# The head of a hybrid encoder block: input tiles loaded first, two scale quarters summed by TensorE from raw blocks, and a new order of the first units

## The chip, the cores and the metric

The kernel runs on one core of a Trainium2 chip. The metric is the device time of one execution in microseconds (us), lower is better; the figures of a kernel are the median, the lowest and the highest of its runs. The profile is one more execution, taken by the hardware profiler.

## What is computed

One layer of an encoder on x with 512 tokens of 1024 features, all in float32. For this change only the beginning matters:

```python
c_act = jax.nn.silu(c)
mods = jnp.split(c_act @ w_ada[l] + b_ada[l], N_MOD, axis=-1)
sh1, sc1, g1, sh2, sc2, g2, sh3, sc3, g3 = mods
h = modulate(rmsnorm(x, norm_g[l, 0]), sh1, sc1)      # h * (1 + sc1) + sh1
x = x + 0.5 * g1[:, None, :] * swiglu(h, w_ffn1_in[l], w_ffn1_out[l])
```

c has 1024 entries, w_ada is 1024 x 9216 (nine vectors of 1024), w_ffn1_in is 1024 x 5632. After that follow the mixer (HGRN2 heads and windowed attention with a relative bias and a sink logit) and a second SwiGLU.

## The kernel before

The 1024 features are eight tiles (d or k, 0 to 7) of 128, features on partitions, tokens on the free axis. A product of float32 accuracy is made of three products of rounded parts: high weight x high activation (`hi_hi`), low weight x high (`lo_hi`), high weight x low (`hi_lo`). ScalarE rounds (`w_hi`, `h_hi`), VectorE subtracts (`w_lo`, `h_lo`). Each engine runs its own list in the order in which it is written out by hand, with waits on semaphores between engines; nothing is planned at run time. All loads named here go through SyncE's queue in program order, except `rows` (biases and gains) and small stores, which ScalarE issues.

**The head** (65 us with unit 2) works up to the first two units of FFN 1 (unit 0 is a gate tile pair, unit 1 the matching up pair):

- `x_nat` (two halves of 1 MB) is turned by TensorE into `xT` (`turn_x`); its root mean square per token goes into `rms0` (`square`, sqrt, reciprocal), `xn` = x / rms is turned as well (`turn_xn`) into banks.
- The factor `fac` of feature tile d is (1 + scale + bias) x gain, and the scale is a column of c_act @ w_ada. It is made in three pieces: tiles 0 and 1 (quarter 0), 2 and 3 (quarter 1), 4 to 7 (half 1). VectorE multiplies each of the eight k blocks by its entry of `cact` and adds them (`quarter_step`, `scale_step`, all in `first_step`), and TensorE sums the result over partitions with a column of ones (`column_sums`). The semaphore `s_mm` counts the pieces made, `s_step` VectorE's steps. `first_factor` then makes `fac`, `first_hi` and `first_lo` the two parts of h for a tile, `first_t` a float32 copy (`tmod`).
- `hi_hi(u, tiles)`, `lo_hi`, `hi_lo` are the products of unit u over these feature tiles, with the shift left out; the shift is made in the same way (`shift_step`) and added later.
- `w_first[0]` and `w_first[1]` hold the weights of units 0 and 1; unit 0's first half is split early (`first_split`), the rest counts in `whi_done` and `wlo_done`.
- The relative bias rows (`relb`, `table`, line 2143) and the sink broadcast (line 2144) are two float32 products that later stages need; ScalarE copies them out as `row8` and `sink_b`.

On TensorE the head stands in this order (lines 2129 to 2232): the turn of `rows`, column sums of quarter 0, turns of x tiles 0 and 1, bias and sink products, turns of xn tiles 0 to 2, unit 0 over tiles 0 and 1, column sums of quarter 1, turns, unit 0 over tiles 2 and 3, unit 1 over tiles 0 to 3, turns, column sums of half 1, and so on to the end of unit 1.

A float32 product of 128 weight columns stands in the trace as two instructions, each with its own weight load: the 2 products of `column_sums` for a quarter are 4 instructions there, the 4 for a half 8. A turn is one instruction per 128 x 128 block, a rounded product one per 128 x 512 block.

Of the kernel before, what the change touches and what calls it, by code (L numbers as in the profile page):

```python
# [108 lines left out]
def build(nc, x, c, w_ada, b_ada, norm_g, w_ffn1_in, w_ffn1_out, w_ffn2_in, w_ffn2_out,  # L109
# [163 lines left out]
    with ctx:  # L273
# [473 lines left out]
        def _(a):  # L747
# [76 lines left out]
            a.wait_ge(rowpad_done, 1)  # L824
            a.dma_start(bias_rows.rearrange("(h j) -> h j", h=QH), row8[:]).then_inc(bias_stored, 16)
            evac_x(2)
            first_t(2)
            first_t(3)
            evac_x(3)
            evac_x(4)  # L830
# [1843 lines left out]
```

## Time and profile before

| | |
|---|---|
| median of 3 runs | 1036.09 us (1035.14 to 1036.89) |
| the profiled execution | 1035.85 us |
| its span, first to last instruction | 1034.0 us |
| outside the span | 1.85 us |
| PE busy | 1013.7 us, 98% of the span |
| VectorE (DVE) busy | 804.1 us, 78% |
| ScalarE (ACT) busy | 507.9 us, 49% |
| the head with units 0 to 2 (line 2038 begins) | 65.4 us |

Busy shares are averages over a thousand microseconds; the change lies in the first 45. So the table says only that TensorE is nearly never idle over the whole kernel, and what the head is worth is to be read from its timeline and its chain.

### The profile page before, as it was taken

The numbers are of one execution on the slowest core, as the hardware profiler recorded it, in microseconds if no ns is written. First come the engines' busy times: TensorE is split into PE (matmuls) and PEld (weight loads), VectorE is DVE, ScalarE is ACT, GpSimd is POOL, SyncE is SP. The second block draws the span as 40 slices with busy tenths as digits, with TensorE's granted clock in tenths as the row PEclk, the third lists the DMA queues.
The fourth block names the chain that finished last, engine by engine and source line by source line (L and its number), as shares of the span: only waits on it lengthen the run. The fifth ranks groups of instructions, "written<-read, shape, count | busy, mean of one in ns | idle before, by whom it ended". The sixth has DMA issues, their size and how long they took to land.

```text
span 1034.0 us, 16712 instructions
## 1 busy us (share of the span) xinstructions
PE 1013.7 (98%) x6238; PEld 897.7 (87%) x6238; DVE 804.1 (78%) x1188; ACT 507.9 (49%) x782; POOL 48.8 (5%) x33
## 2 busy tenths in 40 slices
PE   5999999999999999999999999999999999999998
PEld 3788999999888888878878888887999999988887
DVE  6889989988987789888788649579888888746533
ACT  4646555555222354683535773554555555522231
POOL 0000000000000050020200000320000000000000
PEclk9999999999999999999999999999999999999999
DMA  9643434343877442823120031222232332363312
GB/s 345 233 163 122 133 114 139 105 159 127 294 275 244 163 163 84 273 72 102 41 72 31 2 83 41 82 82 82 83 121 93 110 115 88 123 245 124 119 41 82
DMA packets 93811, 133.59 MB, mean 129 GB/s; under 512 B 10786, under 2 KB 77214, under 8 KB 93639
## 3 DMA queue, kind: packets, MB, share of 16 engines
q1 hardware_dynamic: 93438, 130.83, 38.0%
q10 hardware_dynamic: 328, 2.17, 0.6%
q8 instruction: 28, 0.46, 0.2%
q14 instruction: 17, 0.13, 0.0%
HBM read 130.88 MB, written 4.21 MB: 131 GB/s over the span
## 4 chain that ended last, share of the span: by engine, by line
PE 85%; DVE 8%; ACT 2%; POOL 2%; DMA 2%; issue 1%; SPq 0%; POOLq 0%; DVEq 0%; ACTq 0%
PE bank L2038 13%; PE bank L2040 13%; PE bank L2039 13%; PE bank L2286 11%; PE bank L2285 11%; PE bank L2284 11%; PE bank L2388 2%; DVE w_lo L1254 2%; PE bank L2489 2%; PE bank L2582 1%; PE bank L2475 1%; ACT w_hi L757 1%; PE bank L2175 1%; DVE tmod L1338 1%; PE bank L2161 1%
## 5 line engine op out<-in xcount | busy, mean ns | idle before, releaser
L757 ACT ACTIVATE w_hi<-w_raw 128x2048 fp32r<-128x2048 f32 x47 | 90.0, 1914 | 201.9 <-PE bank L2040 190.9
L1254 DVE TENSOR_TENSOR w_lo<-w_raw,w_hi 128x2048 fp32r<-128x2048 f32 x47 | 109.5, 2330 | 94.6 <-ACT w_hi L757 94.5
L2284 PE MATMUL bank<-t_hi,left_hi 128*128 128x256 f32 x544 | 154.0, 283 | 0.0
L2285 PE MATMUL bank<-t_lo,left_hi 128*128 128x256 f32 x544 | 154.0, 283 | 0.0
L2286 PE MATMUL bank<-t_hi,left_lo 128*128 128x256 f32 x544 | 153.9, 283 | 0.0
L2038 PE MATMUL bank<-a_hi,w_hi 128*128 128x512 f32 x352 | 137.7, 391 | 0.3 <-DVE w_lo L1254 0.3
L2040 PE MATMUL bank<-a_hi,w_lo 128*128 128x512 f32 x352 | 137.0, 389 | 0.0
L2039 PE MATMUL bank<-a_lo,w_hi 128*128 128x512 f32 x352 | 137.0, 389 | 0.0
L2038 PE MATMUL bank<-h_hi,w_hi 128*128 128x512 f32 x336 | 133.3, 397 | 0.8 <-DVE w_lo L1254 0.8
L2040 PE MATMUL bank<-h_hi,w_lo 128*128 128x512 f32 x336 | 130.9, 390 | 0.0
L2039 PE MATMUL bank<-h_lo,w_hi 128*128 128x512 f32 x336 | 130.8, 389 | 0.0
L2286 PE MATMUL bank<-h_hi,left_lo 128*128 128x256 f32 x408 | 115.5, 283 | 0.0
L2285 PE MATMUL bank<-h_lo,left_hi 128*128 128x256 f32 x408 | 115.5, 283 | 0.0
L2284 PE MATMUL bank<-h_hi,left_hi 128*128 128x256 f32 x408 | 115.5, 283 | 0.0
L926 ACT ACTIVATE left_hi<-s_raw 128x512 fp32r<-128x512 f32 x136 | 85.6, 630 | 54.1 <-PE bank L2286 28.5
L2284 PEld LDWEIGHTS bank<-t_hi,left_hi 128*128 128x128 f32 x544 | 104.4, 192 | 0.0
L2285 PEld LDWEIGHTS bank<-t_lo,left_hi 128*128 128x128 f32 x544 | 104.4, 192 | 0.0
L2286 PEld LDWEIGHTS bank<-t_hi,left_lo 128*128 128x128 f32 x544 | 104.4, 192 | 0.0
L1544 DVE TENSOR_TENSOR left_lo<-s_raw,left_hi 128x512 fp32r<-128x512 f32 x136 | 92.9, 686 | 5.0 <-ACT left_hi L926 3.8
L1544 DVE TENSOR_TENSOR left_lo<-w_raw,left_hi 128x512 fp32r<-128x512 f32 x102 | 67.5, 688 | 20.2 <-ACT left_hi L926 18.9
L2284 PEld LDWEIGHTS bank<-h_hi,left_hi 128*128 128x128 f32 x408 | 78.3, 192 | 0.1
L2285 PEld LDWEIGHTS bank<-h_lo,left_hi 128*128 128x128 f32 x408 | 78.3, 192 | 0.1
(313 smaller groups left out, 1893.3 us busy)
## 6 DMA issues: line engine op xcount, KB each, us to landing
w_raw<-in_w_ffn_in SPq DMA_DIRECT2D x42, 1024.0 KB, 4.9
ada<-in_w_ada SPq DMA_DIRECT2D x24, 1024.0 KB, 5.0
w_raw<-in_w_ffn_out SPq DMA_DIRECT2D x22, 1024.0 KB, 4.8
w_raw<-in_w_mix_in SPq DMA_DIRECT2D x11, 1024.0 KB, 5.1
shift_in<-in_w_ada SPq DMA_DIRECT2D x4, 1024.0 KB, 8.3
ada_row<-in_w_ada SPq DMA_DIRECT2D x8, 512.0 KB, 4.2
scale_in<-in_w_ada SPq DMA_DIRECT2D x4, 512.0 KB, 6.9
x_nat<-in_x SPq DMA_DIRECT2D x2, 1024.0 KB, 9.0
```

The source lines that it names most:

```text
L757: sc.activation(w_hi[n % 2][:], src[:], ACT.Copy).then_inc(whi_done, 1)
L926: sc.activation(left_hi[p][:], left_source(f, u, p), ACT.Copy).then_inc(high_done, 1)
L1254: ve.tensor_tensor(w_lo[n % 2][:], src[:], as_f32(w_hi[n % 2][:]), ALU.subtract).then_inc(wlo_done, 1)
L1544: ve.tensor_tensor(left_lo[p][:], left_source(f, u, p), as_f32(left_hi[p][:]), ALU.subtract).then_inc(low_done, 1)
L2038: te.matmul(out_ap, wh, xh, start=first, stop=False)
L2039: te.matmul(out_ap, wh, xl, start=False, stop=False)
L2040: return te.matmul(out_ap, wl, xh, start=False, stop=last)
L2284: te.matmul(into, wh, xh[:, k, :], start=(opens and k == 0), stop=False, skip_group_check=True)
L2285: te.matmul(into, wh, xl[:, k, :], start=False, stop=False, skip_group_check=True)
L2286: ins = te.matmul(into, wl, xh[:, k, :], start=False, stop=(k == 3), skip_group_check=True)
L2388: ins = te.matmul(bank[4 + h][:, cols].rearrange("p (m two j) -> p m two j", two=2, j=b), kc(lev, h // GH)[:, h % GH, cols], alternate(q_b ...
L2489: ins = te.matmul(bank[4 + 2 * (n % 2) + g][:, j * (DH + 1):(j + 1) * (DH + 1)], pT[u % 4][:, i, :], av[:, key_first(n) + i, g, :], start= ...
```

## The change

The loads take a new order: both halves of x before the scale blocks, the first half of unit 0's weights after the first scale quarter, the second half of them last, behind the scale half. The two scale quarters are no longer multiplied and added by VectorE: TensorE multiplies each raw 128 x 128 block (as weights) by a column of `cact` (`direct_sums`), eight blocks for each of four feature tiles, accumulating in PSUM. The bias and sink products move from before the turns of xn to behind the first block of unit 0. Unit 1 over tiles 0 and 1 comes before unit 0 over tiles 2 and 3; `lo_hi(1, ...)` becomes one run before the column sums of the half instead of standing around them. ScalarE's and VectorE's lists follow.

```diff
+        SINK_SUM = bank[7][:, 32:32 + QH]
+        SCALE_SUMS = (bank[7][:, 0:1], bank[0][:, 0:1], bank[7][:, 2:3], bank[7][:, 3:4])
...
-            load_scale(0, 0)
-            load_scale(0, 1)
             for half in range(2):
                 sp.dma_start(x_nat[:, 2 * half:2 * half + 2, :],
...
+            load_scale(0, 0)
+            load_scale(0, 1)
+            load_w(0, slice(0, 4), first_ready[6])
             sp.dma_start(sink_r[:], attn_sink).then_inc(bias_consts, 16)
...
-            load_w(0, slice(0, 4), first_ready[6])
-            load_w(0, slice(4, DT), raw_ready[0])
             load_scale(1, 0)
             load_scale(1, 1)
             load_w(1, everything, raw_ready[1])
             load_scale_half(0)
             load_scale_half(1)
+            load_w(0, slice(4, DT), raw_ready[0])
...
+            square(0)
             a.wait_ge(vec_step, 1)
             sc.activation(vec[:], bank[0][:, 0:P], ACT.Copy).then_inc(vec_step, 1)
-            square(0)
...
-            a.wait_ge(sink_step, 1)
-            sc.activation(sink_b[:], bank[0][:, 0:QH], ACT.Copy).then_inc(sink_step, 1)
             evac_x(0)
+            evac_x(1)
             a.wait_ge(first_ready[6], 16)
...
+            a.wait_ge(sink_step, 1)
+            sc.activation(sink_b[:], SINK_SUM, ACT.Copy).then_inc(sink_step, 1)
             a.wait_ge(bias_mm, 1)
             sc.activation(row8[:], bank[3][0:QH, :], ACT.Copy).then_inc(rowpad_done, 1)
-            evac_x(1)
+            evac_x(2)
+            whi(1)
             first_hi(2)
             first_hi(3)
-            whi(1)
...
-            v.wait_ge(c_step, 2)
-            for k in range(DT):
-                quarter_step(0, k)
+            v.sem_inc(s_step, 16)
             square(1)
             v.wait_ge(vec_step, 2)
             ve.tensor_scalar(modv[:, DT:2 * DT], vec[:, DT:2 * DT], 1.0, None, ALU.add).then_inc(lb_dve, 1)
-            v.wait_ge(lb_dve, 1)
-            v.wait_ge(s_mm, 1)
-            first_factor((0, 1), (bank[7][:, 0:1], bank[7][:, 1:2]))
             square(3)
...
+            v.wait_ge(lb_dve, 1)
+            v.wait_ge(s_mm, 1)
+            first_factor((0, 1), SCALE_SUMS[0:2])
             v.wait_ge(first_split, 1)
             split_first(slice(0, 4 * 2 * P))
             first_lo(0)
             first_lo(1)
-            for k in range(DT):
-                quarter_step(1, k)
-            scale_step(0)
+            v.wait_ge(c_step, 2)
+            v.wait_ge(whi_done, 1)
+            ve.tensor_tensor(w_lo[1][:], w_first[1][:], as_f32(w_hi[1][:]), ALU.subtract).then_inc(wlo_done, 1)
             v.wait_ge(s_mm, 2)
...
+            def direct_sums(q, order):
+
+                for k, i in order:
+                    if i == order[0][1] and k % 4 == 0:
+                        pe.wait_ge(first_ready[2 * q + k // 4], 16)
+                    ins = te.matmul(SCALE_SUMS[2 * q + i], scale_in[q][:, k, i * P:(i + 1) * P], cact[:, k:k + 1],
+                                    start=(k == 0), stop=(k == DT - 1))
+                ins.then_inc(s_mm, 1)
...
+            direct_sums(0, [(k, i) for k in range(DT) for i in range(2)])
             pe.wait_ge(norms[0].rt, 2)
...
+            te.matmul(SINK_SUM, ones[0:1, :], sink_r[:], start=True, stop=True).then_inc(sink_step, 1)
+            te.matmul(bank[3][0:QH, :], relb[:], table[:], start=True, stop=True).then_inc(bias_mm, 1)
+            pe.wait_ge(sink_step, 2)
+            direct_sums(1, [(k, i) for i in range(2) for k in range(DT)])
+            pe.wait_ge(xT_act, 2)
+            pe.wait_ge(rowpad_done, 1)
+            pe.wait_ge(whi_done, 1)
+            hi_hi(1, (0, 1))
+            hi_lo(1, (0, 1))
```

The first place is TensorE's list from the turn of `rows` to the end of unit 0's first block. The numbers behind `quarter_acc` and `scale_in` are the quarters (98 and 89 quarter 0, 99 and 90 quarter 1), `w_hi_77` and `w_lo_79` are unit 0's weights. Before:

```order
L2130 MATMUL bank<-ident,rows 128x128
L2125 MATMUL bank<-ones,quarter_acc_98 128x1 x2
L2112 MATMUL bank<-ident,x_nat 128x128 x8
L2143 MATMUL bank<-table,relb 8x512
L2144 MATMUL bank<-sink_r,ones 128x8
L2112 MATMUL bank<-ident,xn 128x128 x12
L2161 MATMUL bank<-h_hi,w_hi_77 128x512 x4
L2167 MATMUL bank<-h_hi,w_lo_79 128x512 x4
L2175 MATMUL bank<-h_lo,w_hi_77 128x512 x4
L2125 MATMUL bank<-ones,quarter_acc_99 128x1 x2
```

The same stretch of TensorE's list in the change:

```order
L2110 MATMUL bank<-ident,x_nat 128x128 x4
L2141 MATMUL bank<-ident,rows 128x128
L2110 MATMUL bank<-ident,x_nat 128x128 x4
L2132 MATMUL bank<-cact,scale_in_89 128x1 x16
L2110 MATMUL bank<-ident,xn 128x128 x12
L2163 MATMUL bank<-h_hi,w_hi_77 128x512 x4
L2169 MATMUL bank<-h_hi,w_lo_79 128x512 x4
L2177 MATMUL bank<-h_lo,w_hi_77 128x512 x4
```

Two products ahead of the turns of xn have become sixteen, and the bias and sink products are gone from there.

The second place is TensorE's list behind that block, up to the column sums of the scale half (`w_hi_78`, `w_lo_80` are unit 1's weights). Before:

```order
L2112 MATMUL bank<-ident,xn 128x128 x4
L2112 MATMUL bank<-ident,x_nat 128x128 x4
L2161 MATMUL bank<-h_hi,w_hi_77 128x512 x4
L2167 MATMUL bank<-h_hi,w_lo_79 128x512 x4
L2175 MATMUL bank<-h_lo,w_hi_77 128x512 x4
L2161 MATMUL bank<-h_hi,w_hi_78 128x512 x8
L2175 MATMUL bank<-h_lo,w_hi_78 128x512 x8
L2112 MATMUL bank<-ident,xn 128x128 x4
L2112 MATMUL bank<-ident,x_nat 128x128 x8
L2167 MATMUL bank<-h_hi,w_lo_80 128x512 x4
L2125 MATMUL bank<-ones,scale_acc 128x1 x4
L2167 MATMUL bank<-h_hi,w_lo_80 128x512 x4
```

In the change the stretch begins so:

```order
L2110 MATMUL bank<-ident,xn 128x128 x4
L2110 MATMUL bank<-ident,x_nat 128x128 x4
L2193 MATMUL bank<-sink_r,ones 128x8
L2194 MATMUL bank<-table,relb 8x512
L2132 MATMUL bank<-cact,scale_in_90 128x1 x16
L2163 MATMUL bank<-h_hi,w_hi_78 128x512 x4
L2177 MATMUL bank<-h_lo,w_hi_78 128x512 x4
L2163 MATMUL bank<-h_hi,w_hi_77 128x512 x4
```

and ends so:

```order
L2163 MATMUL bank<-h_hi,w_hi_78 128x512 x4
L2177 MATMUL bank<-h_lo,w_hi_78 128x512 x4
L2110 MATMUL bank<-ident,x_nat 128x128 x8
L2169 MATMUL bank<-h_hi,w_lo_80 128x512 x8
L2123 MATMUL bank<-ones,scale_acc 128x1 x4
L2110 MATMUL bank<-ident,xn 128x128 x8
```

Eighteen small products stand ahead of unit 1's first four, and between the scale half's sums and the next unit-0 product only eight turns are left.

The third place is VectorE's list behind `first_lo` of tiles 0 and 1 (`TENSOR_TENSOR w_lo_80` is the low part of unit 1's weights). Before, with the semaphores that each row waits for:

```order
L1372 TENSOR_SCALAR quarter_acc_99<-scale_in_90,cact 128x256 [waits ada_first_ready2]
L1375 SCALAR_TENSOR_TENSOR quarter_acc_99<-scale_in_90,cact,quarter_acc_99 128x256 [waits s_step] x3
L1375 SCALAR_TENSOR_TENSOR quarter_acc_99<-scale_in_90,cact,quarter_acc_99 128x256 [waits s_step,ada_first_ready3]
L1375 SCALAR_TENSOR_TENSOR quarter_acc_99<-scale_in_90,cact,quarter_acc_99 128x256 [waits s_step] x3
L1372 TENSOR_SCALAR scale_acc<-scale_half_91,cact 128x512 [waits ada_first_ready4]
L1396 SCALAR_TENSOR_TENSOR fac<-bank,modv,vec 128x1 [waits s_mm]
L1396 SCALAR_TENSOR_TENSOR fac<-bank,modv,vec 128x1
L1414 SCALAR_TENSOR_TENSOR h_lo<-bank,fac,h_hi 128x512 [waits n0_hi] x2
L1375 SCALAR_TENSOR_TENSOR scale_acc<-scale_half_91,cact,scale_acc 128x512 [waits s_step] x2
L1455 TENSOR_TENSOR w_lo_80<-w_first_102,w_hi_78 128x2048 [waits whi_done]
```

In the change:

```order
L1447 TENSOR_TENSOR w_lo_80<-w_first_102,w_hi_78 128x2048 [waits whi_done,c_step]
L1398 SCALAR_TENSOR_TENSOR fac<-bank,modv,vec 128x1 [waits s_mm]
L1398 SCALAR_TENSOR_TENSOR fac<-bank,modv,vec 128x1
L1416 SCALAR_TENSOR_TENSOR h_lo<-bank,fac,h_hi 128x512 [waits n0_hi] x2
L1374 TENSOR_SCALAR scale_acc<-scale_half_91,cact 128x512 [waits ada_first_ready4]
L1377 SCALAR_TENSOR_TENSOR scale_acc<-scale_half_91,cact,scale_acc 128x512 [waits s_step] x3
```

Eight steps are gone, and the subtraction for unit 1's weights now stands ahead of the second `fac`.

## Rows read from the trace of the kernel before

**Rows 1.** The page, parts 1 and 2: busy time, granted TensorE clock.

```profile
PE 1013.7 (98%) x6238; PEld 897.7 (87%) x6238; DVE 804.1 (78%) x1188; ACT 507.9 (49%) x782; POOL 48.8 (5%) x33
...
PEclk9999999999999999999999999999999999999999
```

**Rows 2.** Stretches of the head: length, busy time per engine, PEclk, DMA share, GB/s.

```profile
13.30:19.90 6.60, 6.16 (x21) 3.73 (x21) 4.77 (x8) 4.99 (x9) 0.00 (x0) 1.00 1.09 387
19.90:27.00 7.10, 5.61 (x24) 4.26 (x24) 5.68 (x13) 3.42 (x7) 0.00 (x0) 1.00 1.05 409
27.00:43.00 16.00, 15.74 (x82) 12.46 (x82) 14.21 (x21) 9.92 (x15) 0.00 (x0) 1.00 0.63 215
```

**Rows 3.** Timeline of PE, 9 to 27 us: start, length of the group, instructions.

```profile
9.76 0.98 PE L2125 MATMUL bank<-ones,quarter_acc 128*128 128x1 f32 x4
...
13.26 1.12 PE L2112 MATMUL bank<-ident,x_nat 128*128 128x128 f32 x4 [1.46 <-DMA x_nat<-in_x]
14.30 1.87 PE L2143 MATMUL bank<-table,relb 33*8 33x512 f32 x2
...
16.63 2.82 PE L2112 MATMUL bank<-ident,xn 128*128 128x128 f32 x12
19.89 2.04 PE L2161 MATMUL bank<-h_hi,w_hi 128*128 128x512 f32 x4 [0.44 <-ACT h_hi L787]
21.73 1.33 PE L2167 MATMUL bank<-h_hi,w_lo 128*128 128x512 f32 x4
22.91 1.07 PE L2175 MATMUL bank<-h_lo,w_hi 128*128 128x512 f32 x4
25.21 0.61 PE L2125 MATMUL bank<-ones,quarter_acc 128*128 128x1 f32 x4 [1.24 <-DVE quarter_acc L1375]
...
27.04 1.30 PE L2161 MATMUL bank<-h_hi,w_hi 128*128 128x512 f32 x4 [0.28 <-ACT h_hi L787]
```

**Rows 4.** Timeline of PE, 31 to 39 us.

```profile
31.84 1.98 PE L2175 MATMUL bank<-h_lo,w_hi 128*128 128x512 f32 x8
...
36.02 1.05 PE L2125 MATMUL bank<-ones,scale_acc 128*128 128x1 f32 x8
...
37.94 1.03 PE L2112 MATMUL bank<-ident,xn 128*128 128x128 f32 x8
38.73 1.32 PE L2161 MATMUL bank<-h_hi,w_hi 128*128 128x512 f32 x4
```

**Rows 5.** Timeline of DVE, 10 to 36 us.

```profile
10.66 1.23 DVE L1408 CUSTOM_DVE_ANT_0 xn<-x_nat 128x1024 f32<-128x1024 f32 x1 [1.05 <-DMA x_nat<-in_x]
...
13.24 1.23 DVE L1408 CUSTOM_DVE_ANT_0 xn<-x_nat 128x1024 f32<-128x1024 f32 x1 [0.88 <-DMA x_nat<-in_x]
...
15.05 2.08 DVE L1440 TENSOR_SCALAR xn<-x_nat,rms 128x1024 f32<-128x1024 f32 x3
...
21.49 3.67 DVE L1375 SCALAR_TENSOR_TENSOR quarter_acc<-scale_in,cact,quarter_acc 128x256 f32<-128x256 f32 x7
...
25.86 0.34 DVE L1396 SCALAR_TENSOR_TENSOR fac<-bank,modv,vec 128x1 f32<-128x1 f32 x2 [0.30 <-PE bank L2125]
...
29.80 2.28 DVE L1455 TENSOR_TENSOR w_lo<-w_first,w_hi 128x2048 fp32r<-128x2048 f32 x1
32.00 3.96 DVE L1375 SCALAR_TENSOR_TENSOR scale_acc<-scale_half,cact,scale_acc 128x512 f32<-128x512 f32 x5
```

**Rows 6.** Timeline of ACT, 19 to 29 us.

```profile
19.06 1.27 ACT L787 ACTIVATE h_hi<-bank,fac 128x512 fp32r<-128x512 f32 x2 [0.72 <-PE bank L2112]
...
21.81 0.57 ACT L817 ACTIVATE row<-bank 8x512 f32<-8x512 f32 x1
...
26.30 0.69 ACT L787 ACTIVATE h_hi<-bank,fac 128x512 fp32r<-128x512 f32 x1 [3.44 <-DVE fac L1396]
...
27.45 1.91 ACT L757 ACTIVATE w_hi<-w_first 128x2048 fp32r<-128x2048 f32 x1
```

**Rows 7.** The last stretch of the span, columns as in group 2.

```profile
1032.00:1034.00 2.00, 0.00 (x0) 0.00 (x0) 0.00 (x0) 0.00 (x0) 0.00 (x0) 0.65 0.52 155
```

More of the change, by code:

```diff
@@ L815, in _ @@
             first_t(1)
+            a.wait_ge(sink_step, 1)
+            sc.activation(sink_b[:], SINK_SUM, ACT.Copy).then_inc(sink_step, 1)
             a.wait_ge(bias_mm, 1)
             sc.activation(row8[:], bank[3][0:QH, :], ACT.Copy).then_inc(rowpad_done, 1)
-            evac_x(1)
+            evac_x(2)
+            whi(1)
             first_hi(2)
             first_hi(3)
-            whi(1)
+            first_t(2)
+            first_t(3)
+            a.wait_ge(rowpad_done, 1)
+            a.dma_start(bias_rows.rearrange("(h j) -> h j", h=QH), row8[:]).then_inc(bias_stored, 16)
+            evac_x(3)
+            evac_x(4)
             a.wait_ge(raw_ready[0], 16)
             sc.activation(w_hi[0][:, 4 * 2 * P:], w_first[0][:, 4 * 2 * P:], ACT.Copy).then_inc(whi_done, 1)
[L824 to L830, printed above, removed]
             first_hi(4)
@@ L1444, in _ @@
             first_lo(1)
-            for k in range(DT):
-                quarter_step(1, k)
-            scale_step(0)
+            v.wait_ge(c_step, 2)
+            v.wait_ge(whi_done, 1)
+            ve.tensor_tensor(w_lo[1][:], w_first[1][:], as_f32(w_hi[1][:]), ALU.subtract).then_inc(wlo_done, 1)
             v.wait_ge(s_mm, 2)
-            first_factor((2, 3), (bank[7][:, 2:3], bank[7][:, 3:4]))
+            first_factor((2, 3), SCALE_SUMS[2:4])
             first_lo(2)
             first_lo(3)
-            scale_step(1)
-            scale_step(2)
-            v.wait_ge(whi_done, 1)
-            ve.tensor_tensor(w_lo[1][:], w_first[1][:], as_f32(w_hi[1][:]), ALU.subtract).then_inc(wlo_done, 1)
+            for k in range(3):
+                scale_step(k)
             for k in range(3, DT):
@@ L2127, in column_sums @@
                 ins.then_inc(s_mm, 1)
-            pe.wait_ge(rows_loaded, 16 * 6)
-            te.transpose(bank[0][:, 0:P], rows[:], ident[:]).then_inc(vec_step, 1)
-            pe.wait_ge(pool_set, 7)
-            column_sums(8, quarter_acc[0], 0, 2)
+            def direct_sums(q, order):
[5 more added lines that the diff above has]
+                ins.then_inc(s_mm, 1)
             pe.wait_ge(x_loaded[0], 16)
@@ L2136, in _ @@
             turn(bank[2], x_nat, 1, (0, 1))
+            pe.wait_ge(rows_loaded, 16 * 6)
+            te.transpose(bank[0][:, 0:P], rows[:], ident[:]).then_inc(vec_step, 1)
             pe.wait_ge(x_loaded[1], 16)
@@ L2139, in _ @@
             turn(bank[2], x_nat, 1, (2, 3)).then_inc(x_tr, 1)
-            pe.wait_ge(bias_consts, 48)
             pe.wait_ge(vec_step, 2)
-            te.matmul(bank[3][0:QH, :], relb[:], table[:], start=True, stop=True).then_inc(bias_mm, 1)
-            te.matmul(bank[0][:, 0:QH], ones[0:1, :], sink_r[:], start=True, stop=True).then_inc(sink_step, 1)
+            direct_sums(0, [(k, i) for k in range(DT) for i in range(2)])
             pe.wait_ge(norms[0].rt, 2)
@@ L2177, in hi_lo @@
                 return ins
-            pe.wait_ge(sink_step, 2)
             pe.wait_ge(xT_act, 1)
@@ L2185, in _ @@
             hi_lo(0, (0, 1))
-            column_sums(16, quarter_acc[1], 2, 2)
             pe.wait_ge(norms[0].t, 1)
@@ L2190, in _ @@
             turn_x(2)
+            pe.wait_ge(pool_set, 7)
+            pe.wait_ge(bias_consts, 48)
+            te.matmul(SINK_SUM, ones[0:1, :], sink_r[:], start=True, stop=True).then_inc(sink_step, 1)
[7 more added lines that the diff above has]
+            hi_lo(1, (0, 1))
             hi_hi(0, (2, 3))
@@ L2193, in _ @@
             hi_lo(0, (2, 3))
-            pe.wait_ge(xT_act, 2)
-            pe.wait_ge(rowpad_done, 1)
-            pe.wait_ge(whi_done, 1)
-            hi_hi(1, range(4))
-            hi_lo(1, range(4))
             pe.wait_ge(xT_act, 3)
             turn_xn(4)
+            hi_hi(1, (2, 3))
+            hi_lo(1, (2, 3))
             pe.wait_ge(norms[0].t, 4)
@@ L2204, in _ @@
             pe.wait_ge(wlo_done, 1)
-            lo_hi(1, (0, 1))
+            lo_hi(1, range(4)).then_inc(first_used, 1)
             column_sums(24, scale_acc, 4)
-            lo_hi(1, (2, 3)).then_inc(first_used, 1)
             pe.wait_ge(xT_act, 5)
```

## The prediction, made before the changed kernel ran

> **What bounds the kernel now.** The page says that TensorE (PE) is busy for 98% of the span [rows 1], so over the whole kernel a delay of PE is a delay of the end. In the head this holds only from some point on, and the stretches show from where: PE is busy for 5.61 of 7.10 us from 19.9 to 27 us, and for 15.74 of 16.00 us from 27 to 43 us [rows 2]. So from 27 us PE sets the pace, and what counts is when it gets there and with how much work left. The timeline of PE shows what it waits for before: the second half of x (13.26 us), ScalarE's first `h_hi` (19.89 us), VectorE's second scale quarter (25.21 us, after 1.24 us idle), and `h_hi` of tile 2 (27.04 us) [rows 3]. Nothing behind 27 us has a stall that takes up a delay, so a shift there is taken as passed on in full.
>
> One more thing is to be seen in group 3: PE is slow at first. The granted clock is listed as full, 1.00, in every stretch of the head [rows 2], but the rows disagree with it: from the start of four 128x512 products to the next row it takes 1.84 us at 19.89 us, of which a part is a wait; the later ones cost (1.98 - 1.07) / 4 = 0.23 us each [rows 3, 4]. The small float32 column products say it more cleanly: four take 0.98 us at 9.76 us and 0.61 us at 25.21 us, eight take 1.05 us at 36.02 us [rows 3, 4]. That is (1.05 - 0.61) / 4 = 0.11 us each at full rate, with a tail of 0.28 us, and (0.98 - 0.3) / 3, about 0.22 us, at half rate; I use 0.213, half of the 0.427 us that a half-rate 128x512 product would take. The change to full rate falls into the second row of unit 0's block (21.73 us: 1.33 us for four, the next four 1.07 us) [rows 3]. Before it PE had been busy without a break from 13.26 to 19.4 us, with turns, the 33-row bias product and the sink, and this did not raise the rate; it rose a little over 2 us into the 128x512 products.
>
> **The change, part by part.** I follow PE, which runs its list in order, and call E the moment at which unit 0's first block (twelve 128x512 instructions) is out: before, 22.91 + 4 x 0.227 = 23.8 us [rows 3].
>
> Loads. The halves of x landed at 10.66 and 13.24 us, 2.58 us for 1 MB, with the DMA engines full at 387 GB/s [rows 2, 5]. With x ahead of the 1 MB of scale quarter 0, x is there at about 8.1 and 10.7 us, and the quarter's two halves at about 11.95 and 13.24 us. xn was finished 17.13 - 13.24 = 3.9 us after the second half of x [rows 5], so now at 14.6 us. Nothing later in the queue is short: unit 1's weights come 2.5 MB later, at about 20 us, and the postponed second half of unit 0's weights at about 26.5 us, needed after 37 us.
>
> First sum on PE. Sixteen products are 32 instructions. They start with the first half quarter at 11.95 us and run without a gap, since the second half lands before the first sixteen are through: 32 x 0.213 = 6.8 us, to 18.8 us. I take PE to stay at half rate through it, as it did through the thin products and turns before. The turns of xn stand behind them in the list and start at 19.0 us instead of 16.63 us [rows 3]: xn waits 4.4 us for PE. The bias and sink products, 2.33 us there before (14.30 to 16.63 us), are gone, and this is in the 19.0. So the early x buys nothing: **+2.4 us**. From there to E all is as before: ten turns, `h_hi` at +2.43 us [rows 3, 6], the block. E becomes 26.2 us.
>
> From E on. Before, the products of unit 0 over tiles 2 and 3 started at 27.04 us, E + 3.2 [rows 3]. Now ahead of them stand: eight turns 0.87 us (eight took 0.79 at 37.94 us [rows 4]); the sink and bias products, half of 2.33 us at full rate, 1.15; 32 instructions of the second sum at 0.11, 3.5; and eight products of unit 1 pulled forward, 8 x 0.227 = 1.81 [rows 4]. That is E + 7.3. But `h_hi` of tile 2 comes later still, by a chain across the engines: the bias product ends at E + 2.2, ScalarE copies `row8` and evacuates x tile 2 (0.5 us each, as the 0.57 us row), then rounds unit 1's weights (1.91 us [rows 6]), to E + 5.1; VectorE's list has the subtraction for these weights (2.28 us, 2.2 to the next [rows 5]) ahead of the second `fac`, so that `fac` starts at E + 7.4 although the sum is there at E + 5.5; from `fac` to PE it takes 27.04 - 25.86 = 1.18 us [rows 3, 5]. So PE starts at **E + 8.55** and idles 1.2 us. Of these 8.55 us 1.81 are work done in advance. Net: 8.55 - 3.2 - 1.8 = **+3.5 us**. A cheaper second sum would not help, since it is not on this chain; a half-rate one would.
>
> The scale half. Before, from the start of its column sums (36.02 us) to the next unit-0 product (38.73 us) were 2.71 us, filled by the sums 0.9, four `lo_hi` 0.9 and eight turns 0.8 [rows 4]. The four `lo_hi` now stand ahead. The path (sums, four `fac`, `h_hi`) stays 2.71 us, the cover shrinks by 0.9: **+0.9 us** of idle. The eight steps of VectorE before it start at E + 9.9, cost about 0.78 us each (3.96 us for five [rows 5]), and end at E + 15.7; PE comes to the sums at E + 16.5, so they are just not late. If they were, each microsecond would count in full.
>
> VectorE. Sixteen steps of 0.5 us (seven in 3.67 us [rows 5]) are gone. Of the first eight none was on the path; the other eight were the 1.24 us wait of PE, which is in the E + 3.2. The rest of the relief lands in waits for `s_mm` and for the weights' rounding, so it counts nothing more. ScalarE's `square(0)` ahead of `vec` costs nothing: `vec` is needed at 11.95 us by the first sum, and both are through by 10.3 us. The later shift loads wait for `s_mm` and `xn_tr` and move with PE, and their users move too.
>
> Sum: 2.4 + 3.5 + 0.9 = **+6.8 us** on the profiled 1035.85 us (span 1034.0 and 1.85 around it), 1042.7 us; the median of the runs, 1036.09, stands 0.24 higher, which I leave within the rounding.
>
> What a thin product costs the rows show: 0.11 and 0.21 us for exactly this form, each instruction with its own 128-column weight load [rows 3, 4]. The Trainium skill (TensorE: Matmul & The Clock Gate, Back-to-back issue gap) gives about 25 ns as the floor of a product with few columns. By it the first sum would be 32 x 0.025 = 0.8 us and the turns would start when xn is ready, at 14.6 us, 2 us earlier than before: -2.0 + 3.5 + 0.9 = +2.4 us, an estimate from that page. The trace does not agree with so low a price.
>
> **The rivals.**
> - The rate rises during the first sum. For it: 6.8 us of instructions back to back, each with a full weight load. Against it: the same kind of continuous row between 13.26 and 19.4 us did not do it. If it rises in mid-sum, around 17 us, the sum ends at 18.0, the turns and the block run at full rate (1.3 and 2.7 us), and E is about 23.1 us: -0.7 + 4.4 = +3.7 us, 1039.6 us (1038.7 to 1040.4 by the moment).
> - The rate falls again behind the first block. From E to E + 5.5 there are only turns, thin products and the second sum. Before, 3.2 us of that kind passed without harm [rows 3]; but at the end of the kernel, when only turns were left, the granted clock fell, 0.65 on average over the last 2 us [rows 7]. Then a rest of the second sum, the eight pulled products and a part of the next block run at half rate: about 1 + 0.4 + 1.3 us more, +9.5 us, 1045.4 us. The Trainium skill (same page, HAM oscillation) warns of this, gaps between bursts of products that put the clock back; no row before shows it in the head.
> - PE at full rate nearly from the start: the first sum ends at 15.0 us, the block at 20.2 us, -3.6 + 4.4 = +0.8 us, 1036.7 us: no change. The rows at 9.76 and 19.89 us speak against it.
> - Faster: the head's end is set by VectorE and not by PE. Then x 2.6 us earlier and eight steps less (4.1 us) count, -6.7 us, the chain behind E gives back 3.5: -3.2 us, 1032.7 us. It decides if VectorE has less idle time than PE between 27 and 43 us; it was busy for 14.21 of 16 us against PE's 15.74 [rows 2], so I give it little.
>
> **How the numbers follow.** Half rate through the first sum, no fall: 0.45. Fall behind the block: 0.20. Rise in mid-sum: 0.17. No change: 0.11. Faster: 0.07. The likeliest gives 1042.7 us, by itself 1041.5 to 1044 (when in the block the rate rises, up to 1 us; 0 to 0.9 us for the scale half). For eight in ten the range takes in the mid-sum rise and the fall: 1037.9 to 1046.5 us. 0.2% is 2.07 us, about what a measurement of this kernel can tell from no change; the first three cases are slower by more, 0.82, with a little of the third kept back: slower 0.81, same 0.12, faster 0.07.
>
> **What would show it.** In the changed profile: 32 instructions of line 2132 at about 0.21 us from 12 to 19 us; the first turn of xn near 19.0 us; the first `h_hi` product near 22.3 us; the second sum at 0.11 us each; VectorE's second `fac` directly behind the subtraction of unit 1's weights, and PE idle for about 1.2 us before unit 0's tiles 2 and 3; about 0.9 us idle behind the scale half's sums; the first product of line 2036 near 72.2 us instead of 65.4. I am wrong if the rate is up before 17 us, if a 128x1 instruction on raw blocks costs less than 0.1 us, or if the delay of the head is not found again at the end.

## The result, and the profile after

The changed kernel takes **1042.08 us** (median of 4 runs, 1041.37 to 1042.87), the kernel before 1036.07 us in the same comparison. The ratio is 1.0059, with a 95% interval of 1.0047 to 1.0071: slower by 6.0 us. The profiled execution is one of 1041.37 us with a span of 1039.6 us, 5.6 us more than before.

Parts 1 and 2 of the page after, to be read beside [rows 1]:

```profile
PE 1023.4 (98%) x6294; PEld 908.7 (87%) x6294; DVE 803.2 (77%) x1172; ACT 507.8 (49%) x782; POOL 49.0 (5%) x33
...
PEclk9899999999999999999999999999999999999999
```

TensorE has 56 instructions and 9.7 us of busy time more, VectorE 16 instructions less. That is the exchange which the change makes: 64 thin instructions on PE in place of 8 and of sixteen steps of VectorE. And one digit of the granted clock is new: the second fortieth of the span, which ends at 52 us, has an 8 where before a 9 stood. Where in it the clock is low, the stretches show (length, busy time of PE, PEld, DVE, ACT, POOL, then PEclk, DMA share, GB/s):

```profile
11.90:20.00 8.10, 8.10 (x39) 8.10 (x40) 3.28 (x6) 2.79 (x4) 0.00 (x0) 1.00 1.08 391
20.00:27.00 7.00, 6.56 (x36) 4.44 (x34) 1.41 (x2) 3.66 (x7) 0.00 (x0) 1.00 1.06 404
27.00:36.00 9.00, 9.00 (x39) 8.08 (x39) 5.85 (x8) 4.61 (x6) 0.00 (x0) 0.62 0.38 142
36.00:46.00 10.00, 9.37 (x56) 7.85 (x55) 6.79 (x14) 3.42 (x6) 0.00 (x0) 1.00 0.23 76
71.00:1039.60 968.60, 961.66 (x5996) 857.37 (x5994) 759.72 (x1104) 471.12 (x727) 47.97 (x22) 1.00 0.36 120
```

Before, the clock stood at 1.00 in every stretch of the head [rows 2]. Now it averages 0.62 from 27 to 36 us, where PE is busy for 9.00 of 9.00 us: the busy time looks perfect, and for three quarters of it (27.7 to 34.5 us) PE runs at 1.2 GHz. The other stretches read 1.00. That can't be trusted before 20.88 us: a group of four turns takes 1.11 us there and 0.60 at 23.79 us, so PE is at half rate while the listing says 1.00, as in the kernel before.

The timeline of PE (start, length of the group, what it is, idle time before it), to be read beside [rows 3, 4]:

```profile
6.90 1.11 PE L2110 MATMUL bank<-ident,x_nat 128*128 128x128 f32 x4 [3.64 <-DMA x_nat<-in_x]
9.41 1.12 PE L2110 MATMUL bank<-ident,x_nat 128*128 128x128 f32 x4
10.82 6.96 PE L2132 MATMUL bank<-cact,scale_in 128*128 128x1 f32 x32 [0.29 <-DMA scale_in<-in_w_ada]
17.64 2.80 PE L2110 MATMUL bank<-ident,xn 128*128 128x128 f32 x12
20.88 1.22 PE L2163 MATMUL bank<-h_hi,w_hi 128*128 128x512 f32 x4 [0.44 <-ACT h_hi L789]
...
23.79 0.60 PE L2110 MATMUL bank<-ident,xn 128*128 128x128 f32 x4
...
25.07 1.02 PE L2194 MATMUL bank<-table,relb 33*8 33x512 f32 x2
26.02 5.50 PE L2132 MATMUL bank<-cact,scale_in 128*128 128x1 f32 x32
31.38 2.05 PE L2163 MATMUL bank<-h_hi,w_hi 128*128 128x512 f32 x4
33.23 1.68 PE L2177 MATMUL bank<-h_lo,w_hi 128*128 128x512 f32 x4
34.74 1.08 PE L2163 MATMUL bank<-h_hi,w_hi 128*128 128x512 f32 x4
...
44.99 1.22 PE L2163 MATMUL bank<-h_hi,w_hi 128*128 128x512 f32 x4 [0.63 <-ACT h_hi L789]
71.57 0.39 PE L2036 MATMUL bank<-h_hi,w_hi 128*128 128x512 f32 x1
```

The three landmarks of the prediction: E, the end of unit 0's first block, is at 23.79 us, where it was before (23.8). Unit 0's products over tiles 2 and 3 begin at 34.74 us instead of 27.04. The head ends at 71.57 us instead of 65.40, +6.17 us. The same 128x512 products cost 1.08 us a group of four from 34.74 us, 2.05 at 31.38 us: there the half rate is visible in the rows too.

VectorE and ScalarE, whose rows answer to [rows 5, 6]:

```profile
11.62 2.08 DVE L1437 TENSOR_SCALAR xn<-x_nat,rms 128x1024 f32<-128x1024 f32 x3
17.90 0.34 DVE L1398 SCALAR_TENSOR_TENSOR fac<-bank,modv,vec 128x1 f32<-128x1 f32 x2 [4.19 <-PE bank L2132]
29.09 2.29 DVE L1447 TENSOR_TENSOR w_lo<-w_first,w_hi 128x2048 fp32r<-128x2048 f32 x1 [6.91 <-ACT w_hi L759]
31.55 0.34 DVE L1398 SCALAR_TENSOR_TENSOR fac<-bank,modv,vec 128x1 f32<-128x1 f32 x2 [0.17 <-PE bank L2132]
```

```profile
20.05 1.27 ACT L789 ACTIVATE h_hi<-bank,fac 128x512 fp32r<-128x512 f32 x2 [5.36 <-PE bank L2110]
26.13 0.59 ACT L820 ACTIVATE row<-bank 8x512 f32<-8x512 f32 x1 [0.77 <-PE bank L2194]
27.10 1.89 ACT L759 ACTIVATE w_hi<-w_first 128x2048 fp32r<-128x2048 f32 x1
```

xn is ready at 13.7 us and waits until 17.64 us for PE. The relieved VectorE stands idle for 4.19 us in front of the first `fac` and 6.91 us in front of `w_lo`. So the time that it was spared shows as waiting.

### The profile page after: what moved, and what is told of

It reads as the page before. It is cut to its first block, busy times and chain, and to the rows that moved or that the text cites. A ratio compares the mean times of both kernels' runs of the same rounds, so it can differ in the third digit from the quotient of the medians.

```text
span 1039.6 us, 16807 instructions
## 1 busy us (share of the span) xinstructions
PE 1023.4 (98%) x6294; PEld 908.7 (87%) x6294; DVE 803.2 (77%) x1172; ACT 507.8 (49%) x782; POOL 49.0 (5%) x33
## 4 chain that ended last, share of the span: by engine, by line
PE 89%; DVE 7%; ACT 1%; issue 1%; DMA 1%; SPq 0%; DVEq 0%; ACTq 0%
PE bank L2036 14%; PE bank L2038 14%; PE bank L2037 14%; PE bank L2293 11%; PE bank L2292 11%; PE bank L2291 11%; PE bank L2395 2%; PE bank L2496 2%; PE bank L2589 1%; DVE w_lo L1256 1%; PE bank L2163 1%; PE bank L2132 1%; PE bank L2177 1%; PE bank L2482 1%; PE bank L2169 1%; DVE tmod L1340 1%
## 5 line engine op out<-in xcount | busy, mean ns | idle before, releaser
L2036 PEld LDWEIGHTS bank<-a_hi,w_hi 128*128 128x128 f32 x352 | 66.1, 188 | 14.2 <-DVE w_lo L1256 0.7
```

The source lines that it names most:

```text
L2036: te.matmul(out_ap, wh, xh, start=first, stop=False)
```

## The experiments

Each kernel was timed beside the kernel before, in 5 to 11 runs; the median of the kernel before was 1035.86 to 1035.95 us in these comparisons. The table orders them by what they start from. "Head" is the start of the first product of `stage_k8` in the profiled execution (65.40 us in the kernel before), E and "tiles 2/3" are the landmarks above.

| kernel | E | tiles 2/3 | head | median us | ratio (95%) |
|---|---|---|---|---|---|
| before | 23.8 | 27.04 | 65.40 | 1036.07 | |
| after | 23.79 | 34.74 | 71.57 | 1042.08 | 1.0059 (1.0047 to 1.0071) |
| e1_first_sum_cut | 19.98 | 30.43 | 67.77 | 1037.37 | 1.0016 (1.0007 to 1.0024) |
| e2_second_sum_cut | 24.01 | 33.02 | 70.45 | 1040.56 | 1.0048 (1.0035 to 1.0061) |
| e3_second_sum_dve | 24.12 | 33.12 | 71.07 | 1040.66 | 1.0045 (1.0032 to 1.0058) |
| e9_fill_wait | 24.66 | 32.01 | 68.91 | 1038.78 | 1.0031 (1.0019 to 1.0042) |
| e4_spin | 21.88 | 31.68 | 69.64 | 1040.50 | 1.0046 (1.0033 to 1.0059) |
| e5_old_tail | 25.33 | 29.38 | 69.19 | 1038.35 | 1.0022 (1.0013 to 1.0031) |
| e6_old_tail_spin | 22.25 | 26.30 | 66.17 | 1035.74 | 0.9999 (0.9990 to 1.0008) |
| e8_spin_fill | 25.59 | 29.89 | 69.44 | 1039.08 | 1.0020 (1.0011 to 1.0029) |
| e12_loads_only | 27.5 | 30.69 | 69.05 | 1039.40 | 1.0039 (1.0025 to 1.0052) |
| e10_bias_moved | 23.4 | 26.57 | 64.99 | 1035.60 | 0.9998 (0.9989 to 1.0007) |
| e11_bias_moved_spin | 21.6 | 25.95 | 65.41 | 1035.63 | 1.0000 (0.9991 to 1.0009) |
| e7_before_spin | 22.7 | 26.90 | 66.43 | 1035.45 | 0.9990 (0.9981 to 0.9999) |

Taken within one execution, the time of the profiled run less its head is 969.8 to 970.5 us for all fourteen kernels: a delay of the head is passed on to the end, within 0.8 us. A median can differ from the profiled execution by more (e5's was profiled in the slowest of its eleven runs, at 1039.05 us), so a difference is given by medians here, and by profiles where that is said.

**Which sum is on the path.** Two kernels keep the change and cut one of its two sums down to 4 of its 32 instructions, behind a wait for the same loads.

```diff
-            direct_sums(0, [(k, i) for k in range(DT) for i in range(2)])
+            pe.wait_ge(first_ready[1], 16)
+            direct_sums(0, [(0, i) for i in range(2)], 1)
```

> The changed kernel with the first direct sum cut from 32 instructions to 4 (only the first of the eight k blocks is multiplied, so the scale of tiles 0 and 1 is incomplete). Theory, the first sum lies whole on the path: xn is ready at 13.7 us and its turns start there and not at 17.6 us, and the kernel ends 3.0 to 4.0 us earlier than the changed one, at about 1038.5 us, still 2 to 3 us above the kernel before. Rival, the sum is covered by something else (weights, w_hi, the clock): the end moves by less than 1 us.

It measured 4.7 us less than after, a little above the 3.0 to 4.0 expected; by the two profiles it is 3.8. The turns of xn start at 13.32 us instead of 17.64:

```profile
12.48 0.99 PE L2132 MATMUL bank<-cact,scale_in 128*128 128x1 f32 x4 [1.69 <-DMA scale_in<-in_w_ada]
13.32 2.80 PE L2110 MATMUL bank<-ident,xn 128*128 128x128 f32 x12
```

The 28 missing instructions would have taken 28 x 0.213 = 6.0 us; 1.69 us of that is the wait for the second half of the quarter, now uncovered, and the 4.3 us that are left are found at the turns. The first sum stands wholly on the path.

The second kernel does the same to `direct_sums(1, ...)`, with a wait on `first_ready[3]`.

> The changed kernel with the second direct sum cut from 32 instructions to 4 (one of eight k blocks, so the scale of tiles 2 and 3 is incomplete). Theory, the chain bias product, row8, w_hi, w_lo, fac is next behind it: products of unit 0 over tiles 2 and 3 start 8.5 us after the first block's end and not 11 us, PE idles about 4 us in two places, and the kernel ends about 2.4 us earlier than the changed one, about 1039.7 us. Rival, only PE's time counts: 4.9 us of sum and 1.5 us of half-rate products go, 6.4 us, about 1035.7 us.

It measured 1.5 us less than after, so most of the second sum's 5.36 us was hidden, as the first theory has it. The size was 0.9 us off. PE's timeline shows the wait that takes its place:

```profile
26.24 0.61 PE L2132 MATMUL bank<-cact,scale_in 128*128 128x1 f32 x4
29.47 2.05 PE L2163 MATMUL bank<-h_hi,w_hi 128*128 128x512 f32 x4 [2.62 <-ACT w_hi L759]
31.31 1.91 PE L2177 MATMUL bank<-h_lo,w_hi 128*128 128x512 f32 x4
33.02 1.65 PE L2163 MATMUL bank<-h_hi,w_hi 128*128 128x512 f32 x4
```

The pulled-forward products of unit 1 wait 2.62 us for ScalarE's rounding of its weights. VectorE's second `fac` starts at 31.52 us, E + 7.5, directly behind `w_lo`. And the products of unit 1 run at half rate (2.05 and 1.91 us for four): the clock falls here without a second sum.

**The second sum back on VectorE, its `fac` ahead of `w_lo`.**

```diff
-            v.wait_ge(whi_done, 1)
-            ve.tensor_tensor(w_lo[1][:], w_first[1][:], as_f32(w_hi[1][:]), ALU.subtract).then_inc(wlo_done, 1)
+            for k in range(DT):
+                quarter_step(1, k)
             v.wait_ge(s_mm, 2)
             first_factor((2, 3), SCALE_SUMS[2:4])
+            v.wait_ge(whi_done, 1)
+            ve.tensor_tensor(w_lo[1][:], w_first[1][:], as_f32(w_hi[1][:]), ALU.subtract).then_inc(wlo_done, 1)
...
-            direct_sums(1, [(k, i) for i in range(2) for k in range(DT)])
+            column_sums(16, quarter_acc[1], 2, 2)
```

> The changed kernel with quarter 1 summed by VectorE again (eight steps of 0.5 us and two column sums), and the second fac ahead of the subtraction for unit 1's weights. Theory: the VectorE steps run while it would idle (7 us before its w_lo), fac waits no longer for w_lo, the clock has no long thin stretch in which to fall; ScalarE's rounding of unit 1's weights (to 5.1 us behind the block) is then what h_hi of tile 2 waits for, products over tiles 2 and 3 start some 6 us behind the block, and the end is about 5 us earlier than the changed kernel, 1037 us, within 0.2% of the kernel before. Rival, the second sum is not what costs: less than 2 us.

Only 1.4 us less than after, so this was a miss. `fac` comes at 26.99 us and is no longer in the way, but PE's own list is: unit 1's products stand ahead. PE waits 2.62 us for `w_hi`, then runs them at half rate, and tiles 2 and 3 start at E + 9.0 and not at about E + 6:

```profile
26.37 0.58 PE L2125 MATMUL bank<-ones,quarter_acc 128*128 128x1 f32 x4
29.57 2.05 PE L2165 MATMUL bank<-h_hi,w_hi 128*128 128x512 f32 x4 [2.62 <-ACT w_hi L759]
31.42 1.91 PE L2179 MATMUL bank<-h_lo,w_hi 128*128 128x512 f32 x4
33.12 1.91 PE L2165 MATMUL bank<-h_hi,w_hi 128*128 128x512 f32 x4
```

**Is it the clock?** e9 takes e3 and puts three products of a constant tile (each two instructions) into this wait.

```diff
             column_sums(16, quarter_acc[1], 2, 2)
+            pe.wait_ge(xT_act, 2)
+            for _ in range(3):
+                te.matmul(bank[2][:], ones[:], ones[:, 0:1].to_broadcast([P, TOK]), start=True, stop=True)
             pe.wait_ge(xT_act, 2)
```

> The kernel of e3_second_sum_dve with three extra 512-column products of ones (2.6 us at full rate) behind the column sums of quarter 1, where PE idled for 2.6 us until unit 1's weights were rounded. Theory, it is the thin and idle stretch behind the block, 5 us and more without 512-column products, in which the rate falls, and two stretches at half rate over real products cost 3.4 us: with the gap filled the rate stays up and the median falls from 1040.7 to about 1037.3 us. Rival, the fall has another cause or costs nothing: 1040.7 us or more.

It measured 1.9 us less than e3 with more work on PE. The stretch from 27 to 36 us, e3 first, then e9:

```profile
27.00:36.00 9.00, 6.43 (x16) 5.08 (x17) 6.78 (x10) 4.80 (x7) 0.00 (x0) 0.62 0.37 142
```

```profile
27.00:36.00 9.00, 9.00 (x38) 6.33 (x39) 6.34 (x9) 5.35 (x7) 0.00 (x0) 1.00 0.37 140
```

The granted clock is 0.62 in the one and 1.00 in the other. The timeline of PE in e9:

```profile
27.36 2.83 PE L2201 MATMUL bank<-ones 128*128 128x512 f32 x6
30.12 1.15 PE L2165 MATMUL bank<-h_hi,w_hi 128*128 128x512 f32 x4
31.11 1.07 PE L2179 MATMUL bank<-h_lo,w_hi 128*128 128x512 f32 x4
32.01 1.07 PE L2165 MATMUL bank<-h_hi,w_hi 128*128 128x512 f32 x4
```

The products of unit 1 start 0.55 us later than in e3 and are through 1.11 us sooner. So the fall is a cost of its own in this place. Two profiles alone would not show this, since in e9 the clock also rose later within the first block (E is 24.66 us, 24.12 in e3); but all seven runs of e9 (1037.88 to 1039.32 us) lie below all five of e3 (1039.96 to 1040.85).

**The fall without the new tail.** e5 keeps the new loads and the first sum, and puts everything behind the first block into the order of before, except that the bias and sink products stay behind the block.

```diff
-            direct_sums(1, [(k, i) for i in range(2) for k in range(DT)])
-            pe.wait_ge(xT_act, 2)
-            pe.wait_ge(rowpad_done, 1)
-            pe.wait_ge(whi_done, 1)
-            hi_hi(1, (0, 1))
-            hi_lo(1, (0, 1))
+            column_sums(16, quarter_acc[1], 2, 2)
             hi_hi(0, (2, 3))
             lo_hi(0, (2, 3))
             hi_lo(0, (2, 3))
```

> The changed kernel's loads and first sum on PE, and everything behind the first block of unit 0 as before (quarter 1 by VectorE, unit 0 over tiles 2 and 3 ahead of unit 1, ScalarE's rounding of unit 1's weights behind h_hi 2 and 3); bias and sink products stay behind the block. Theory, the tail order and its chain cost the changed kernel its 6 us and loads plus first sum cost nothing: products over tiles 2 and 3 start 4.0 us behind the block's end of 23.8 us, the rate does not fall since the thin stretch is 4 us and not 7.5, and the median is 1036 to 1037 us. If the rate falls all the same, it costs up to 3.4 us: 1039 to 1040 us. Rival, the first sum is the cost: 1040 us or more with no fall in the granted clock.

1038.35 us: with the loads, the first sum and the moved bias products alone the kernel is 2.4 us slower than before, and the new tail costs the other 3.6 of the 6.0. The start of tiles 2 and 3 came as expected, 4.05 us behind the block, but two parts missed: loads and first sum are not free, and the rate fell although the stretch without 128x512 products was 4 us long and not 7.6. In its timeline the full rate comes late, within the second row of the block (from 23.02 us), and tiles 2 and 3 start at E + 4.05:

```profile
21.17 2.04 PE L2166 MATMUL bank<-h_hi,w_hi 128*128 128x512 f32 x4 [0.44 <-ACT h_hi L789]
23.02 1.55 PE L2172 MATMUL bank<-h_hi,w_lo 128*128 128x512 f32 x4
...
29.38 1.31 PE L2166 MATMUL bank<-h_hi,w_hi 128*128 128x512 f32 x4 [1.22 <-ACT h_hi L789]
30.53 1.62 PE L2172 MATMUL bank<-h_hi,w_lo 128*128 128x512 f32 x4
31.95 1.91 PE L2180 MATMUL bank<-h_lo,w_hi 128*128 128x512 f32 x4
```

The clock falls within the row at 30.53 us, and the last row is at half rate: the granted clock is 0.81 from 27 to 36 us, low from 30.9 to 34.3 us. From the first of tiles 2 and 3 to the turns behind unit 1 (37.58 us) it takes 8.20 us, where before it took 6.62 [rows 3] (27.04 to 33.66 us), so the fall is 1.6 us of the 3.8 us by which this profile's head is longer. How much of the 2.4 us of the medians is the fall, no run separates.

Up to this block e5 and after have the same instructions on PE, and their turns of xn start within 0.3 us of each other; yet the block takes 4.16 us in the one and 2.91 in the other, and E differs by 1.5 us. When the rate rises varies that much between two executions.

**The loads alone.** e12 is the kernel before with only the order of loads changed.

```diff
-            load_scale(0, 0)
-            load_scale(0, 1)
             for half in range(2):
                 sp.dma_start(x_nat[:, 2 * half:2 * half + 2, :],
...
+            load_scale(0, 0)
+            load_scale(0, 1)
+            load_w(0, slice(0, 4), first_ready[6])
```

> The kernel before with the change's order of loads alone. Theory, without the sums on PE the early x is of no use: VectorE starts quarter 0's eight steps at 10.7 us instead of 5.5 us and squares and xn follow only then, PE waits with its column sums until 14.8 us, so h_hi comes about 2 us later, 1038 to 1039 us. Rival, the early x counts by itself: 1034 us.

+3.5 us, 0.4 more than the upper end expected. x first, and PE waits for VectorE instead, whose eight steps now stand behind the later quarter:

```profile
15.23 0.98 PE L2125 MATMUL bank<-ones,quarter_acc 128*128 128x1 f32 x4 [5.66 <-DVE quarter_acc L1375]
...
20.28 2.82 PE L2112 MATMUL bank<-ident,xn 128*128 128x128 f32 x12
```

The turns of xn start 3.65 us later than before, and tiles 2 and 3 also 3.65 us later. So the direct sum on PE makes the new load order bearable (e5, +2.4). Not run were the direct sum with the old loads, and the new loads with VectorE's squares ahead of its eight steps; what either costs is open.

**The bias products alone.** e10 is the kernel before with the bias and sink products behind the first block.

```diff
-            te.matmul(bank[3][0:QH, :], relb[:], table[:], start=True, stop=True).then_inc(bias_mm, 1)
-            te.matmul(bank[0][:, 0:QH], ones[0:1, :], sink_r[:], start=True, stop=True).then_inc(sink_step, 1)
...
             hi_lo(0, (0, 1))
+            te.matmul(SINK_SUM, ones[0:1, :], sink_r[:], start=True, stop=True).then_inc(sink_step, 1)
+            te.matmul(bank[3][0:QH, :], relb[:], table[:], start=True, stop=True).then_inc(bias_mm, 1)
```

> The kernel before with one part of the change alone: bias and sink products behind unit 0's first block (the sink sum in bank 7), their copies on ScalarE behind h_hi of tiles 3 and 2. They then fill the 1.2 us in which PE waits for quarter 1, and the turns of xn start at 15.8 us and not at 16.6 us. Theory: about 1 us earlier than before, 1035.0 us. Rival, the block starts in an earlier state of the clock or quarter 1's loads decide: no difference.

> The kernel of e10_bias_moved with the four extra products of ones at the start. Theory: the spin gave e7_before_spin 0.5 us, and here again about 0.5 us, 1034.5 us. Rival: more time without dense products, one more fall, 1036 us.

Head 0.4 us shorter in e10's profile, no difference in either time. The turns of xn start at 16.11 us, held up by ScalarE's part of xn and not by the products. So moved into PE's wait for VectorE they are free, and they were nearly free before. In e11 the block runs at full rate nearly from its start, but the clock falls again, from 25.6 to 29.0 us, over the products of tiles 2 and 3 (2.08 us for the first four, 1.30 in e10): the rival's fall is there, and the head ends where it did before.

**Full rate from the start.** Four kernels let PE run four products of a constant tile (`spin(1)`, and `spin(3)` behind the transposition of `c_row`) while it waits for the first loads: after, e5, before and e10 with this.

```diff
+            pe.wait_ge(pool_set, 2)
+            spin(1)
             pe.wait_ge(consts_loaded, 32)
             te.transpose(bank[2][:, 0:DT], c_row[:], ident[0:DT, 0:DT]).then_inc(c_step, 1)
+            spin(3)
```

> The changed kernel with four extra 512-column products of ones into an unused bank at the very start, while PE waits for the first loads. Theory, half rate is half the price of the first sum: if the rate is up when the sum starts at 10.8 us, its instructions cost 0.11 us and it ends 3.4 us earlier, and the kernel ends 2 to 4 us earlier, about 1039 us; if the rate falls within the sum, less. Rival, instructions on raw blocks are bound by their weight loads at any rate: the sum stays 6.8 us and the end does not move.

> The kernel of e5_old_tail with the four extra products of ones at the start. Theory, the half rate of the first sum and the first block is worth 3 us: if the rate is up at 10.6 us the sum ends at 14.6 us and the block 3 us earlier, 1033 to 1034 us; the rate can fall in the sum, and then half of that is lost, 1035 us. Rival, no gain against e5_old_tail.

> The kernel before with the same four extra products at the start and nothing else. Theory, only the stretch from 13.3 to 22.3 us gains from a full rate: turns, bias product and half of the first block, 1 to 3 us in all, but VectorE's second quarter follows its h_lo and so moves along: 1034 to 1035 us, and nothing if the rate has fallen again by 13 us, where PE waits for x. Rival, the weights and x decide and not the rate: no difference from before.

The gain is 1.6 us on after (its runs spread from 1038.14 to 1041.66), 2.6 on e5, 0.5 on before and none on e10. What limits it is seen in e6. PE's timeline, then its stretches:

```profile
10.92 4.13 PE L2143 MATMUL bank<-cact,scale_in 128*128 128x1 f32 x32 [0.76 <-DMA scale_in<-in_w_ada]
14.91 2.80 PE L2121 MATMUL bank<-ident,xn 128*128 128x128 f32 x12
18.16 2.04 PE L2174 MATMUL bank<-h_hi,w_hi 128*128 128x512 f32 x4 [0.44 <-ACT h_hi L789]
20.00 1.49 PE L2180 MATMUL bank<-h_hi,w_lo 128*128 128x512 f32 x4
```

```profile
14.90:20.00 5.10, 4.66 (x18) 3.90 (x18) 3.40 (x7) 2.44 (x4) 0.00 (x0) 0.50 1.08 395
27.00:31.00 4.00, 4.00 (x12) 3.20 (x12) 3.96 (x5) 4.00 (x5) 0.00 (x0) 0.59 0.91 325
```

The first sum takes 4.0 us instead of 6.8, because most of it runs at full rate. Then the clock falls at 14.0 us, so the turns and the first row of the block are as slow as in e5, and it falls once more behind the block, as in e5. The gain at the sum is kept and nothing is added to it: E, tiles 2 and 3 and the head are 3.1, 3.1 and 3.0 us earlier than in e5. On before it is otherwise. In e7 the block is through 1.1 us earlier, but tiles 2 and 3 still wait for VectorE and start at 26.90 us, and now the clock is low from 26.7 to 30.2 us, where before it was not: the four products there take 2.07 us instead of 1.30, and in this profile the head is 1.0 us longer, though the median is 0.5 us lower.

e8 puts four products of 256 columns into e6's first sum, to hold the clock up through it.

```diff
-                for k, i in order:
+                for n, (k, i) in enumerate(order):
+                    if n % 4 == 2:
+                        spin(1, 2 * P)
```

> The kernel of e6_old_tail_spin with four more products of ones, 256 columns wide, spread over the first sum. Theory, they keep the rate up through the sum for 1.7 us of their own time: the turns of xn then start near 16 us but run with the first block at full rate, and the end is 0 to 1 us earlier than in e6_old_tail_spin. Rival, the rate falls as before and they only cost: 1.7 to 3.4 us later than e6_old_tail_spin.

3.3 us more than e6. The clock fell all the same and was low from 12.6 to 22.8 us, earlier and longer than in e6 (14.0 to 20.9), and the filler had to be paid for at half rate. The rival expectation held.

No version is clearly faster than the kernel before; e7 is the nearest, with 0.9990 and an interval that ends just short of 1 (0.9981 to 0.9999).

## Why the prediction was right, and where its terms were not

The forecast, 1042.7 us, is 0.6 us above the median. The direction and its reasons hold: PE sets the pace, the first sum holds up the turns, the chain behind the block is longer, VectorE's relief is worth nothing. But that the total is so close is luck: two errors of 2.4 us cancel. What happened is not the likeliest case, no fall of the clock, whose number was met, but the rival with a fall, which was put at 1045.4 us.

**Loads and first sum, predicted +2.4 us to E, measured 0.0.** The price was right: 32 instructions from 10.82 to 17.64 us, 0.213 us each. The start was not. It was forecast for 11.95 us and came at 10.82, since x landed by 6.9 and 9.4 us and not at 8.1 and 10.7. With 0.2 us less between sum and turns, xn's turns start at 17.64 us instead of 19.0, so 1.0 us later than before. And the block took 2.91 us from its first product, where before it took 3.9: the full rate came within its first row and not in its second, 1.0 us. 1.4 + 1.0 = 2.4 us, the whole term. The second part is no merit of the change: it differs from one execution to the next. Five profiles have this list up to here (after, e2, e3, e9, e5), and their E is 23.79, 24.01, 24.12, 24.66 and 25.33 us, so the term is 0.0 to 1.5 us. e1 shows what the sum is worth on the path, 3.8 us by the profiles and 4.7 by the medians.

**E to tiles 2 and 3, predicted E + 8.55, measured E + 10.95.** The work on PE was listed right: turns, sink and bias 2.2 us (2.0 predicted), second sum 5.36 (3.5), products of unit 1 3.36 (1.81). The two that are larger ran for the most part at half rate: 17 of the 32 instructions of the sum at 0.213 instead of 0.11 are 1.8 us. So PE had no idle time, where 1.2 us were forecast: 0.2 + 1.9 + 1.5 - 1.2 = 2.4. The chain itself stands: `fac` at 31.55 us, E + 7.8 against 7.4, and in e2, where no sum is in its way, at E + 7.5. By the chain tiles 2 and 3 could have begun 1.18 us behind `fac`, at 32.7 us, E + 8.9; the other 2.0 us are the fall of the clock. e9 against e3 prices the same fall at 1.9 us.

**The rival "the rate falls again", chance 0.20.** It is what happened, in its place, and it should have had more. The argument against it was that 3.2 us of turns and thin products had passed without harm [rows 3]; but the changed kernel has 7.6 us of that kind there, with no 128x512 product before 31.38 us, and the clock fell at 27.7 us, 3.9 us into it. The argument for it misread its row: in the last 2 us of the kernel before, PE ran no turns either, it was idle [rows 7], so that fall says nothing on turns. Its price, 2.7 us on top, was near: 2.0, since the clock was back at about 34.5 us, before the next block. In the Trainium skill (TensorE: Matmul & The Clock Gate, HAM oscillation) the harm comes from time in which PE is idle between bursts. This trace goes further: in after PE has no wait between 20.88 and 34.74 us by its rows, and the clock fell all the same; in e3 there is a wait of 2.62 us, and with the wait filled, in e9, it stayed up.

**The scale half, predicted +0.9 us of idle, measured 0.63** in front of 44.99 us. From tiles 2 and 3 to this product were 11.69 us before [rows 3, 4], now 10.25 and the 1.81 done in advance, 12.06: +0.4 net.

**Sum:** 0.0 + 5.9 + 0.4 = 6.3 us against the 6.17 us read at the end of the head, of which 0.6 are found again behind it (968.0 us from there to the end, 968.6 before): 5.6 in the span.

**The other rivals.** A rise in mid-sum did not occur: 6.96 us for 32 instructions. "Faster, since VectorE ends the head" is refuted by its waits of 4.19 and 6.91 us. The low price for a thin product did not come: the same 32 instructions cost 0.213 us each at half rate, and about 0.11 in e6's first part. The 25 ns of the Trainium skill (same page, Back-to-back issue gap) are a floor for the product without its weight load, as that section says itself, and each instruction here has a weight load of its own.

**What stays open.** What makes the clock rise or fall in the head at one moment and not another was not settled: after and e5 differ with the same list, and e8's filler did not hold it. Beside e9, three profiles list no fall in the head: before, e10 and e12. In them tiles 2 and 3 follow 3.2 us behind the block, and in e5 to e8 and e11, in which the clock fell, 4.1 to 4.3 us behind it; no run changed this distance alone. How much the new tail costs by its longer chain and how much by the fall is known from one profile of after (3.9 and 2.0 us), not from a kernel with this tail in which the clock stays up. That x landed 1.1 us earlier than a shift by 1 MB explains is measured, not explained.

## What to carry to other kernels

Before work is moved from an engine that has slack to the one that sets the pace, price it at the rate that engine has there: 32 instructions of one column each cost 6.8 us here to replace eight steps of VectorE (4.0 us), and for 3.9 us they held up tiles that were ready. Thin products, turns and waits did not keep TensorE's clock up in ten of these fourteen traces, even where its busy share reads 100%; when a reordering puts many of them in a row, look at the granted clock of the stretch behind. Wide products in the wait kept it up and paid (e9), narrower ones spread between thin products did not (e8). And take a change apart: here the new loads alone cost 3.5 us, and with the first sum and the moved bias products still 2.4, a fall of the clock included.
